# Row stores on another queue and four matmul groups moved earlier in a macaron S5/Conformer block

## The reference, cut to what matters

```python
# D_MODEL = SEQ = 1024, BATCH = DEPTH = 1, D_FF = 2816, float32
h = rms_norm(x, norm_ffn1_g);  x = x + 0.5 * swiglu_ffn(h, w_ffn1_up, w_ffn1_down)
h = rms_norm(x, norm_mix_g);   proj = h @ w_in
u_ssm, v_conv, gate_logits = split(proj)
y_ssm = s5_ssm(u_ssm, ...)                     # 64 groups of 16 channels, 64 complex states each
glu_val, glu_gate = split(gelu(y_ssm) @ w_ssm_glu);  y_a = glu_val * sigmoid(glu_gate)
z = causal_depthwise_conv31(val * sigmoid(gate)) + b_dw
y_b = silu(layer_norm(z, ln_g, ln_b)) @ w_pw   # mean and variance over the channels
x = x + (sigmoid(g_A) * y_a + sigmoid(g_B) * y_b) @ w_out
h = rms_norm(x, norm_ffn2_g);  x = x + 0.5 * swiglu_ffn(h, w_ffn2_up, w_ffn2_down)
return rms_norm(x, norm_final_g)
```

## Time and profile before

| | |
|---|---|
| median of 3 runs | 2243.33 us (2242.39 to 2245.36) |
| profiled execution | 2242.39 us, its span 2240.6 us |
| PE busy | 2192.9 us (98% of the span), 10370 matmuls |
| DVE, ACT, POOL busy | 1620.6, 963.4, 620.6 us |
| chain that ended last | PE 84%, DVE 8%, ACT 3%, DMA 3%, issue 2% |
| mean granted TensorE clock | 0.998 |
| DMA | 370.62 MB, mean 165 GB/s |

### The profile page before, as it was taken

How to read it: one execution, slowest core, us unless ns; L and a number is a source line. 1 busy time by engine, 2 the same in 40 slices (tenths; PEclk the granted TensorE clock), 3 DMA queues, 4 the chain that set the end, 5 groups by cost and what they waited for, 6 DMA issues and landing times.

```text
span 2240.6 us, 32120 instructions
## 1 busy us (share of the span) xinstructions
PE 2192.9 (98%) x10370; PEld 1811.8 (81%) x10370; DVE 1620.6 (72%) x2065; ACT 963.4 (43%) x1573; POOL 620.6 (28%) x720
## 2 busy tenths in 40 slices
PE   7999999999999999999999999999999999999998
PEld 6788888888888888888888788888878888887886
DVE  5867777755564999999998659454587787766667
ACT  5455555544554222222223224134355555544444
POOL 2888998700000000000000430000026663531000
PEclk9999999999999999999999999999999999999999
DMA  5223444367763345445435632553257765648654
GB/s 170 78 85 125 145 139 147 126 214 242 248 218 127 103 140 155 132 140 155 138 113 172 197 104 80 192 193 118 71 165 248 252 232 186 221 163 305 211 195 172
DMA packets 299581, 370.62 MB, mean 165 GB/s; under 512 B 26489, under 2 KB 198609, under 8 KB 299120
## 3 DMA queue, kind: packets, MB, share of 16 engines
q1 hardware_dynamic: 279280, 296.04, 41.6%
q0 software_dynamic: 19056, 69.42, 8.5%
q10 hardware_dynamic: 1168, 4.20, 0.5%
HBM read 259.73 MB, written 107.50 MB: 164 GB/s over the span
## 4 chain that ended last, share of the span: by engine, by line
PE 84%; DVE 8%; ACT 3%; DMA 3%; issue 2%; SPq 1%; DVEq 0%; ACTq 0%
PE PU L1347 10%; PE PU L1349 10%; PE PU L1348 10%; PE PU L1288 9%; PE PU L1290 8%; PE PU L1289 8%; PE PU L1227 3%; PE PU L1228 3%; PE PU L1229 3%; PE PD L1227 3%; PE PD L1229 3%; PE PD L1228 3%; PE PD L1423 1%; PE PD L1424 1%; PE PD L1425 1%
## 5 line engine op out<-in xcount | busy, mean ns | idle before, releaser
L1288 PE MATMUL PU<-Hhi,Whi 128*128 128x512 f32 x896 | 352.7, 394 | 2.6 <-DVE Hlo L2386 2.0
L1289 PE MATMUL PU<-Hlo,Whi 128*128 128x512 f32 x896 | 349.2, 390 | 0.0
L1290 PE MATMUL PU<-Hhi,Wlo 128*128 128x512 f32 x896 | 349.2, 390 | 0.0
L2365 DVE SCALAR_TENSOR_TENSOR XT<-XT,wq 128x1024 f32<-128x1024 f32 x240 | 313.2, 1305 | 8.2
L1288 PEld LDWEIGHTS PU<-Hhi,Whi 128*128 128x128 f32 x896 | 168.3, 188 | 40.8 <-issue 3.0
L1290 PEld LDWEIGHTS PU<-Hhi,Wlo 128*128 128x128 f32 x896 | 168.3, 188 | 35.0
L1289 PEld LDWEIGHTS PU<-Hlo,Whi 128*128 128x128 f32 x896 | 168.4, 188 | 34.8 <-issue 0.7
L1347 PE MATMUL PU<-Hhi,Dhi 128*128 128x512 f32 x480 | 187.2, 390 | 1.9 <-ACT s1b L1696 1.9
L1348 PE MATMUL PU<-Hlo,Dhi 128*128 128x512 f32 x480 | 187.0, 390 | 0.0
L1349 PE MATMUL PU<-Hhi,Dlo 128*128 128x512 f32 x480 | 186.9, 389 | 0.0
L1227 PE MATMUL PD<-Dhi,Ahi 128*128 128x512 f32 x352 | 138.4, 393 | 5.6 <-DVE Alo L2010 5.6
(11 more groups left out here) (416 smaller groups left out, 5218.2 us busy)
## 6 DMA issues: line engine op xcount, KB each, us to landing
d_act<-G SPq DMA_DIRECT2D x88, 256.0 KB, 2.1
XT<-in_w_ffn_down SPq DMA_DIRECT2D x88, 256.0 KB, 3.2
XT<-d_act SPq DMA_DIRECT2D x88, 256.0 KB, 3.4
Wraw<-in_w_ffn_up SPq DMA_DIRECT2D x80, 256.0 KB, 4.2
XT<-in_w_ffn_up SPq DMA_DIRECT2D x80, 256.0 KB, 4.4
Wraw<-in_w_in SPq DMA_DIRECT2D x32, 512.0 KB, 5.2
Wraw<-d_sb SPq DMA_DIRECT2D x55, 256.0 KB, 2.9
d_sb<-TAB POOLq DMA_DIRECT2D x21, 512.0 KB, 3.2
```

Of the source, the lines that this page charges most:

```text
L1288: mm(o_, Whi[s][:, side, k, :], Hhi[:, k, hs[h]], start=k == 0, stop=False)
L1289: mm(o_, Whi[s][:, side, k, :], Hlo[:, k, hs[h]], start=False, stop=False)
L1290: last = mm(o_, Wlo[s][:, side, k, :], Hhi[:, k, hs[h]], start=False, stop=k == KT - 1)
L2365: stt(CVb, z_, w_, CVb, ALU.mult, ALU.add).then_inc(m["conv"], 1)
```

## The change

The four stores of the finished first-half rows move from ACT's queue to SP's: SP now issues them (`store_rows`, L484) behind its load of step 3 of phase 2, each after a wait on DVE's second add of that row tile, in FFN1 and in the output projection. The residual loads of the output projection stand behind the load of step 6 instead of step 7. On PE, `kernel_of_chunk(7)` stands before the half pair instead of behind its tile 2, `s5_outputs(7)` stands before the first two GLU tiles instead of behind them, and the mean and the two variance products stand two tiles earlier each.

```diff
@@ SP
         for p in range(4):
             proj_phase(sp, FFN1, p, load_step if p else first_steps,
                        [{20: lambda: load_rows(FFN1, 0, x_rows)}, {3: mix_first},
-                        {3: lambda: mix_pair(0, 1), 20: next_rows}, {}][p])
+                        {3: lambda: (store_rows(FFN1, 0, d_x), mix_pair(0, 1)), 20: next_rows}, {}][p])
@@ SP
             proj_phase(sp, OUTP, p, lambda S, p, t: None if p == 0 and t < RING else load_step(S, p, t),
-                       {0: {7: residuals}}.get(p, {}))
+                       {0: {6: residuals}, 2: {3: lambda: store_rows(OUTP, 0, d_x2)}}.get(p, {}))
@@ PE, mix
-            pair_half(q * 2 + (R_MIX + 1), 1, 0, mix_ready, {2: lambda: kernel_of_chunk(q)} if end else {})
+            if end:
+                kernel_of_chunk(q)
+            pair_half(q * 2 + (R_MIX + 1), 1, 0, mix_ready)
             if not end:
                 kernel_of_chunk(q)
@@ PE, behind mix(7)
+        s5_outputs(KT - 1)
         pair_waits(R_GLU, 0)
-        pair_tiles(R_GLU, 0, 0, glu_ready, range(2))
-        s5_outputs(KT - 1)
-        pair_tiles(R_GLU, 0, 0, glu_ready, range(2, KT - 1))
+        pair_tiles(R_GLU, 0, 0, glu_ready, range(KT - 1))
@@ PE
-        glu(1, ({}, {7: ln_mean}, {}, {}))
-        glu(2, ({4: lambda: ln_var(0)}, {6: lambda: ln_var(1)}, {}, {}))
+        glu(1, ({}, {5: ln_mean}, {}, {}))
+        glu(2, ({2: lambda: ln_var(0)}, {4: lambda: ln_var(1)}, {}, {}))
@@ ACT, squares
-                if p == 1:
-                    act.dma_start({FFN1: d_x, OUTP: d_x2}[S][j], xo(S, 0, j)).then_inc(x_st, 16)
```

## The result

The changed kernel is slower: 2260.04 us, median of 6 timed runs (2258.05 to 2262.33), against 2242.98 us for the kernel before in the runs beside them (2242.39 to 2245.36). The ratio is 1.0075, 95% interval 1.0061 to 1.0088: 17 us more, where 9.4 were forecast and the range ended at 2256.5. The direction was right, the size was half.

What follows compares the result with a forecast made beforehand. PE was taken to bound the kernel, so only its waits count: 1.95 + 2.4 + 2.7 + 3.0 - 0.3 - 1.1 = 8.65 us, with the clock 9.4, for a median of 2252.7 us; range 2247.5 to 2256.5.

Steps and rivals of the forecast that it cites:

- Mean product: Layer norm's mean product two tiles earlier: PE waits for POOL's last sums before the second half, +1.95 us.
- second variance: Layer norm's second variance product two tiles earlier: PE arrives before POOL's sum and waits, +2.4 us.
- first variance: Layer norm's first variance product two tiles earlier: uses 2.7 of 8.5 us of slack, costs nothing.
- Residual rows: Output projection, phase 0: step 7's load lands behind the residual rows; PE waits 4.2 us, phase 1's wait goes, +2.7 us.
- queue rival: Small loads are not held up: step 7 and FFN1's step 4 land in time, +1.8 us, 2245.1 us; chance 0.09.
- FFN1's stores: FFN1, phase 2: SP waits for DVE's adds, so step 4 lands late and PE waits, +3.0 us.
- The output projection's stores: Output projection, phase 2: the last store leaves 1.9 us sooner, but step 4's load is behind the stores; gain 0.3 us.
- Last chunk: Mix's last chunk into the GLU: DVE's 1.96 us wait ends, PE idles 2.4 us before S5's outputs; gain 1.1 us.
- Sum of the waits: All edits of the change together, without the clock term: 8.65 us more.
- The clock: Half-clock loss behind the new long waits at step 7 and FFN1: +0.8 us, half of one 1.5 us loss; bounds 0 and 3.0.
- Waits up to 1.96 us show none of this: Kernel before: only its 3.95 us wait was followed by half clock, losing 1.5 us; waits up to 1.96 us were not.
- clock rival: The clock falls at both long waits, step 7's and FFN1's: 8.65 + 3.0 = 11.7, 2255.0 us; chance 0.22.

Runs made afterwards that it cites:

- e7_ffn1_late: Kernel before, with FFN1's four row stores on SP's queue but behind its load of step 12 instead of step 3: 2242.36 us, ratio 0.9997.
- e4_chunk: Kernel before, with only the last chunk's edits: S5 kernel product before the half pair, S5 outputs before the GLU tiles; 2243.71 us, ratio 1.0000.
- e9_all_fill: Changed kernel with thrown-away matmuls on PE in its five new waits: 2252.06 us, ratio 1.0037 to the kernel before.
- e3_ffn1_store: Kernel before, with only FFN1's four row stores on SP's queue, behind its load of step 3 of phase 2: 2249.02 us, ratio 1.0016.
- e12_after_again: Changed kernel run once more without an edit, on another chip than the filled one: 2260.24 us, ratio 1.0074 to the kernel before.

## Why the forecast was half right

- **Mean product, +1.95, and second variance, +2.4**: right. The waits are 2.05 and 2.21 us, released by POOL's sums as worked out. The first variance waits for nothing.
- **Residual rows, +2.7**: right. SP issued them at 1502.29 and the load of step 7 at 1503.34, which landed 13.1 us later, at 1516.4, 14.1 us behind the residual issue as before. The wait is 4.06 us (forecast 4.2), and that of the earlier trace rows is gone, so 2.73. The queue rival is refuted: the small load did not get past the large ones.
- **FFN1's stores, +3.0**: right, 2.87 and 2.94 in two kernels, and e7_ffn1_late shows the cause that was named, the standing SP. That it fits to 0.1 us is in part luck: step 4's weights landed at 589.8 and its activations at 590.4, where the forecast had 591.0, and from there to PE's start it took 1.5 us instead of 1.3.
- **The output projection's stores, -0.3**: right: 1.5 us became 1.16.
- **Last chunk, -1.1**: right in its mechanism: DVE's wait of 1.96 us is gone, and the S5 outputs start 29.7 us behind the transposed table instead of 30.8. The size is shown to about 1 us only (e4_chunk). It gathers the gap into one of 2.60 us, which can lose what was won. The forecast saw the gap of 2.4 and priced no clock behind it.
- **Sum of the waits, 8.65**: right within what can be told; 8.5 us with the clock held up (e9_all_fill).
- **The clock, +0.8 with bounds 0 and 3.0**: this is the term that failed, at the sentence "Waits up to 1.96 us show none of this" and the step from it. Measured: 7 to 8 us (8.3 by the ratios with and without filling, 8.4 by the mean clock with the waits counted in). Three things were wrong in it. The wait for step 7 was as long as the one in the earlier trace rows, which lost 1.5 us, yet the forecast added half of that. The sentence was drawn from one execution, and in others the same kind of wait, of 1.88 us, is followed by half clock (e3_ffn1_store, e12_after_again). And the price of one fall was taken as the 1.5 us of a 3 us window; the stretches are 3.4 or 6.8 us long, and lose 1.5 to 3.0 us each. Five waits of 2 to 4.2 us are five possible falls, which at up to 3.0 us puts the upper bound at 15 us instead of 3.0.

The clock rival (0.22, 2255.0 us) had the right mechanism, but allowed it at the two long waits alone and at 3.0 us together. How often a fall comes can be counted in the fourteen profiles of all the kernels here, over PE's single waits of 1.3 us and more between its first 40 us and its last matmuls:

| PE's wait, us | waits | followed by half clock |
|---|---|---|
| 1.31 to 1.86 | 21 | 0 |
| 1.88 to 1.98 | 19 | 10 |
| 2.04 to 2.97 | 16 | 11 |
| 3.01 to 4.31 | 9 | 9 |

The same wait in the same place goes either way: that of 1.88 us at the transposes behind FFN1, which the change doesn't touch, is followed by half clock in 5 of 12 profiles. The Trainium skill (TensorE: Matmul & The Clock Gate, Why this matters for your kernels) draws the limit at gaps above about 3 us. All nine such waits here agree with it; the 21 falls behind shorter ones don't, and there the measurement decides.

What decides whether the clock falls behind a wait between 1.88 and 2.97 us stays open. The work around it is the same in every execution, and no run was made to vary it.

## What to carry to other kernels

Price a new wait on a busy TensorE with its length and, as an upper bound, with the half-clock stretch behind it, and not only for the longest (1.88 us was enough here), and take that price from several executions. Where such a wait has to stay, matmuls on operands that are there can keep the clock: behind what was left of the five waits, 0.2 to 1.1 us, it stayed at 1.00. And before an order is given to another engine's queue, ask what stands behind its wait: the same stores cost 3.6 us (by the ratio; 4.8 by the means) ahead of the loads of step 4 and nothing that can be told behind those of step 12.

## What was not expected of the hardware

- The granted clock fell to 0.50 in 21 of 35 waits of 1.88 to 2.97 us, for 3.4 or 6.8 us; the same wait in the same kernel did and did not bring it (2.60 us at the S5 outputs: 1.00 behind it at 2256.33 us, 0.58 in the 2264.0 us execution).
- The clock explains little of the spread of the kernel before from run to run: over its 84 executions beside the experiments (2238.41 to 2246.93), the 8 with a mean clock of 0.996 took 2244.1 us on average and the 7 with 0.999 took 2242.6. What makes up the rest is open.
- Matmuls with thrown-away results, 53 of them or some 12 us of PE inside waits, cost nothing that shows and gave back 8 us (4 to 13 by the intervals).
